# GpSimd makes the first weight sum of every up item that is made by quarter products

## The reference

```python
def swiglu(h, w13, w2):
    g, u = jnp.split(h @ w13, 2, axis=-1)
    return (jax.nn.silu(g) * u) @ w2

for l in range(DEPTH):
    h = modulated_norm(x, norm_w[l, 0], mod[:, 0])
    x = x + 0.5 * mod[:, 0, 2, None] * rmsnorm(swiglu(h, ffn_w13[l, 0], ffn_w2[l, 0]), norm_w[l, 1])
    ...
    h = modulated_norm(x, norm_w[l, 4], mod[:, 2])
    x = x + 0.5 * mod[:, 2, 2, None] * rmsnorm(swiglu(h, ffn_w13[l, 1], ffn_w2[l, 1]), norm_w[l, 5])
```

## Time and profile before

| | |
|---|---|
| median of 3 runs | 2648.08 us (2647.03 to 2648.61) |
| the profiled execution | 2643.59 us, span 2641.9 us |
| TensorE matmul busy | 2527.2 us, 96% |
| TensorE weight loads busy | 1893.2 us, 72% |
| VectorE busy | 1817.5 us, 69% |
| ScalarE busy | 516.6 us, 20% |
| GpSimd busy | 242.4 us, 9% |
| chain that ended last | TensorE 72%, VectorE 18%, DMA 3% |

### The profile page before, as it was taken

One profiled execution on the slowest core, in us unless ns is written; L12 is line 12 of the kernel. 1 busy time (PEld: TensorE's weight loads), 2 busy tenths in 40 slices (PEclk: granted clock), 3 DMA queues, 4 the chain that ended last, 5 costly groups with the idle time before them and its releaser, 6 DMA issues.

```text
span 2641.9 us, 69930 instructions
## 1 busy us (share of the span) xinstructions
PE 2527.2 (96%) x31413; PEld 1893.2 (72%) x31413; DVE 1817.5 (69%) x3017; ACT 516.6 (20%) x1053; POOL 242.4 (9%) x372
## 2 busy tenths in 40 slices
PE   7999999999999999999999999999999999999998
PEld 6984877877775455499579758787778745556993
DVE  4786455667785876479879865556787758664765
ACT  1000232212221332110010011322222223321000
POOL 6200101000001101010000010110010011010000
PEclk9999999999999999999999999999999999999999
DMA  9985433322235552398577654423222275435543
GB/s 362 323 298 176 136 114 104 118 86 94 94 109 198 177 192 96 127 314 282 197 255 276 223 173 142 157 86 104 100 89 86 95 242 171 172 112 178 197 160 127
DMA packets 239004, 445.34 MB, mean 169 GB/s; under 512 B 8920, under 2 KB 103702, under 8 KB 238704
## 3 DMA queue, kind: packets, MB, share of 16 engines
q1 hardware_dynamic: 224016, 395.60, 43.0%
q0 software_dynamic: 12960, 38.98, 4.6%
q10 hardware_dynamic: 1728, 6.29, 0.6%
HBM read 422.88 MB, written 17.96 MB: 167 GB/s over the span
## 4 chain that ended last, share of the span: by engine, by line
PE 72%; DVE 18%; DMA 3%; issue 3%; ACT 2%; SPq 1%; POOL 1%; DVEq 0%; POOLq 0%; ACTq 0%
PE ps L1230 71%; DVE scratch L2505 10%; DVE scratch L2511 3%; DMA ring<-in_ffn_w 2%; DVE scratch L2508 1%; DVE ring L2505 1%; DVE gbc L2511 1%; DMA scratch<-acs_scratch 1%; PE ps L1259 1%; DVE scratch L2937 1%; DVE x L2511 0%; DMA acs_scratch<-scratch 0%; ACT scratch L2149 0%; PE ps L1947 0%; DVE merged L2505 0%
## 5 line engine op out<-in xcount | busy, mean ns | idle before, releaser
L1230 PE MATMUL ps<-scratch 64*64 64x32 f32 (+6 forms) x15928 | 785.0, 245 | 62.2 <-DVE scratch L2505 27.6
L1230 PEld LDWEIGHTS ps<-scratch 64*64 64x64 f32 (+2 forms) x15928 | 635.3, 141 | 246.1 <-issue 116.3
L1230 PE MATMUL ps<-hT,ring 64*64 64x256 f32 (+3 forms) x8096 | 784.6, 356 | 9.5 <-issue 3.3
L1230 PEld LDWEIGHTS ps<-hT,ring 64*64 64x64 f32 (+2 forms) x8096 | 636.4, 155 | 89.5 <-issue 17.8
L1230 PE MATMUL ps<-ring,hT 64*64 64x256 f32 (+2 forms) x2816 | 425.4, 423 | 5.5 <-DVE scratch L2511 2.6
L2505 DVE TENSOR_TENSOR scratch<-scratch 128x256 f32<-128x256 f32 (+5 forms) x557 | 339.0, 609 | 108.7 <-ACTq L2313 31.8
L1230 PE MATMUL ps<-ring,scratch 128*128 128x512 f32 x864 | 394.1, 594 | 2.5 <-DVE scratch L2508 1.3
L1230 PEld LDWEIGHTS ps<-ring,hT 64*64 64x64 f32 (+1 forms) x2816 | 229.1, 150 | 142.8 <-issue 115.9
L1230 PEld LDWEIGHTS ps<-ring,scratch 128*128 128x128 f32 x864 | 158.3, 190 | 172.2 <-issue 166.6
L2505 DVE TENSOR_TENSOR scratch<-scratch,ps 128x512 f32<-128x512 f32 (+2 forms) x385 | 195.6, 508 | 116.3 <-PE ps L1230 89.7
L2511 DVE SCALAR_TENSOR_TENSOR scratch<-scratch,ccol 128x1024 f32<-128x1024 f32 x120 | 154.7, 1289 | 15.5 <-DMA scratch<-in_ada_w 11.4
(11 more groups left out here) (248 smaller groups left out, 1759.9 us busy)
## 6 DMA issues: line engine op xcount, KB each, us to landing
ring<-in_w_in SPq DMA_DIRECT2D x56, 2048.0 KB, 8.9
ring<-in_ffn_w SPq DMA_DIRECT2D x88, 1024.0 KB, 7.7
scratch<-in_ada_w SPq DMA_DIRECT2D x66, 1024.0 KB, 10.2
ring<-in_ffn_w SPq DMA_DIRECT2D x80, 512.0 KB, 5.6
ring<-in_w_branch_mamba SPq DMA_DIRECT2D x8, 2048.0 KB, 8.0
scratch<-acs_scratch POOLq DMA_DIRECT2D x24, 512.0 KB, 6.2
scratch<-fill_scratch SPq DMA_DIRECT2D x16, 512.0 KB, 8.5
ring<-in_w_branch_rwkv SPq DMA_DIRECT2D x4, 2048.0 KB, 10.8
```

The lines of the kernel that those rows point to most:

```text
L1230: return pe.matmul(o, lhsT, rhs, start=start, stop=stop)
```

## The change

GpSimd gets a helper, `first_weight_sums`, which for each item waits for the weights and, where the buffer was in use, for the quarter product m5 of item j - 2 that read it, then makes s1 = a21 + a22. VectorE waits for that instead of the weights and makes the three other sums. In GpSimd's order the calls stand: in block (l, 0) ahead of the roots of the norms (l, 2) and (l, 3), which in layer 0 is behind `constants()`; in block (0,1) two items behind `layer_parameters`, eight behind `layer_rows`; in block (1,1) all ten behind the load into `merged`.

```diff
+        first_sum_made = signal("first_sum_made", 0)
...
+            def first_weight_sums(l, f, js):
+
+                for j in js:
+                    item = ffn_item(f, j)
+                    par = item % 2
+                    w = ring[:, par, :].rearrange("p (k u n) -> p k u n", k=KT, u=2)
+                    pool.wait_ge(*slot_loaded[par](l, loads_before(item, par) + 2))
+                    if seven((l, f), j - 2):
+                        pool.wait_ge(*product(l, f, f"m5_{j - 2}"))
+                    pool.tensor_tensor(kset[j % 2][0], w[:, 0:KT // 2, 1, :], w[:, KT // 2:KT, 1, :], ALU.add).then_inc(first_sum_made.sem, 1)
...
                     last_gate_row(0)
                     constants()
+                first_weight_sums(l, 0, SEVEN[l, 0])
                 rstd((l, 2), (l, 3))
...
                     layer_parameters(l + 1)
+                    first_weight_sums(l, 1, SEVEN[l, 1][:2])
                     pool.wait_ge(*made(l, 1, "act_1"))
                     layer_rows(l + 1)
+                first_weight_sums(l, 1, SEVEN[l, 1][2 if l + 1 < DEPTH else 0:])
...
                 dve.wait_ge(*slot_loaded[par](l, loads_before(item, par) + 2))
-                own.step(tt(s1, a21, a22, ALU.add))
+                dve.wait_ge(*first_sum_made(0, seven_count(l, f, j)))
                 own.step(tt(a21, a11, a21, ALU.subtract))
```

More of the change, by code:

```diff
@@ L210, in up_count, with seven_count @@
     return sum(len(names(b)) for b in before) + names((l, f)).index(name) + 1
+def seven_count(l, f, j):
+    before = BLOCKS[:BLOCKS.index((l, f))]
+    return sum(len(SEVEN[b]) for b in before) + SEVEN[l, f].index(j) + 1
 def up_read(l, f, j):
```

## The result

The changed kernel takes 2662.03 us (median of 4, 2657.69 to 2663.93) where the kernel before takes 2647.56 beside it (4 runs, 2643.36 to 2648.61): ratio 1.0055, 95% interval 1.0041 to 1.0069, slower by 14.5 us. The prediction had 2663.0. The profiled execution took 2663.93, its span is 2661.9. In the rows PE is TensorE, PEld its weight loads, DVE VectorE, ACT ScalarE and POOL GpSimd.

The account below looks back on a forecast made before the run. The prediction took TensorE (96% busy) as the bound, with VectorE nearly in balance in the middle blocks' up phases. Terms 9.1 + 2.5 + 0.9 + 4 - 1.5 = +15.0 us on the median 2648.08 gave 2663 us, range 2654 to 2676.

Parts of the forecast that it names:

- Item 2's wait: Block (0,0), fourth quarter product of item 2: TensorE waits 9.1 us for a sum queued behind GpSimd's constants.
- The clock: Behind TensorE's wait at item 2 of (0,0): work at half clock speed costs 2.5 us.
- The end of (0,0): Down sums of block (0,0): the last item's sum comes later and VectorE passes it on, 0.9 us.
- Block (0,1): Block (0,1): item 1's wait plus collisions, less slack and what the last two give back, +4 us (-2.8 to +10).
- six of eight landings collide at +1.1 each: Items 3 to 10 of (0,1): six weight landings put GpSimd's addition on VectorE's pieces or weight sums, +1.1 us each.
- Item 1's own wait: Block (0,1), item 1: the sum waits behind GpSimd's parameter loads, costing TensorE 1 us.
- Block (1,0): Block (1,0): VectorE's load ends +1.0 over eight items, early savings go into the 2.7 us wait; -1.5 us.
- the good bound (-4.1): Block (1,0), favourable end of the range: the 2.7 us wait and its slow clock gone, -4.1 us.
- Block (1,1): Block (1,1): no pieces after the fourth item and TensorE doesn't wait, so 0 us.
- the constants stay slow: Rival, start of (0,0): constants don't speed up, wait 16.4 instead of 9.1 us, +22.3, 2670 us; chance 0.20.
- every addition collides: Rival, blocks (0,1) and (1,0): all 16 landings cost 1.1 us, +31, 2679 us; chance 0.08.
- VectorE relieved: Rival: VectorE keeps its pace beside GpSimd and its waits go, +4.0, 2652 us, within 0.2%; chance 0.10.

Follow-up runs that it names:

- e3: Changed kernel, but GpSimd makes item 2's sum of block (0,0) inside its building of constants, ahead of the fifth selecting step; 2650.86 us.
- e2: Kernel before, but GpSimd makes the first weight sum of item 2 of block (0,0) alone, the other 34 stay on VectorE; 2654.89 us.
- e4: Changed kernel, but GpSimd's sum for item 1 of block (1,0) waits until that block's first normalised tile is made; 2656.43 us.
- e11: Changed kernel, but for item 1 of block (1,0) GpSimd copies a21 instead of adding a21 and a22; no time given.
- e12: Changed kernel, but for item 1 of block (1,0) GpSimd fills the tile with zeros instead of adding; no time given.
- e1: Changed kernel, but VectorE again makes the first weight sum of item 2 of block (0,0), GpSimd keeps the other 34; 2651.09 us.
- e9: Changed kernel with item 2's sum made inside the constants and item 1's sum of (1,0) held until the normalised tile; 2645.77 us, ratio 1.0000.
- e10: Changed kernel, but GpSimd makes each sum as two halves of 128x512; 2662.30 us.

## Why the prediction was right, and where not

The forecast of +15.0 us met +14.5. For the largest term, item 2 and the clock behind it, that is earned: 11.6 in the sum, 12.8 by the rows. That the total is so close is luck: the terms of (0,1) and (1,0) erred by 5.4 and 2.2 us, in opposite directions; the steps add up to 13.7, and the interval of the measured difference is 11 to 18 us.

- **Item 2's wait, 9.1:** 9.6. The constants ended at 73.07 where I had 73.8, and the product could start at 79.63 where I had 80.2. The wait is longer all the same, as TensorE was ready at 70.0 in this execution and not at 71.13. Right, with its reason (e3 shows the slow selects coming back), within the 8.0 to 9.7 that the wait takes in e2, e4, e11 and e12.
- **The clock, 2.5:** 3.1 (6.17 us of matmuls at the half level). The bound taken from the earlier trace rows, 5.5 us at half speed, was too short by a little.
- **The end of (0,0), 0.9:** a step of 1.6, and 3.4 to 6.5 in the seven other kernels with these additions (e1, e3, e4, e9 to e12), where the wait is 2.4 to 4.7 and the clock drops too. The term was mis-sized: I counted the 1.1 us of the last item's later sum and set the earlier items at nothing behind their whole items. With them on GpSimd the last landing came 0.2 to 3 us later. The changed kernel's profile shows the smallest of these steps.
- **Block (0,1), +4:** -1.4, of which 1.0 is in e2 too. The step that failed is "six of eight landings collide at +1.1 each". Of items 3 to 10 three met an operation that they held (the additions at 1174.24, 1188.54 and 1251.58), none of them a weight sum; the other five fell on closing sums, which read PSUM, one of them on the end of a weight sum too, and lengthened none of these. In the block VectorE had 5.5 us less to do. Item 1's own wait was foreseen at 1 us and is 0.86. A collision at its worst is a little larger than I took it, 2.6 us and not 2.35, for instance on a group of four multiplications that takes 5.25 undisturbed:

```profile
1172.44 7.89 DVE L2532 SCALAR_TENSOR_TENSOR scratch<-scratch,ccol 128x1024 f32<-128x1024 f32 x4
...
1174.24 2.36 POOL L1046 TENSOR_TENSOR scratch<-ring 128x1024 f32<-128x1024 f32 x1
```

  My walk through the landings kept VectorE at the pace of before, while in fact each miss or hit moves it against the next one. That this is why fewer met such an operation is my reading; no run shows it.
- **Block (1,0), -1.5:** +0.7, from two parts. At its end -4.4, the good bound (-4.1) whole, against a load that I had growing by 1.0; over items 2 to 10 it fell by 3.8 (11.0 us of sums against four operations longer by 7.2). At its start +5.1, which the sum didn't have at all. In the list of what each addition could meet I only had VectorE's sums and pieces; item 1's addition stands directly behind the statistic and one transfer in GpSimd's queue, and the normalisation waits for that same statistic, so the two start together. Asking which of VectorE's operations GpSimd itself releases would have shown it.
- **Block (1,1), 0:** the shift stays at 20.2 to 20.3 us through it. Four of its ten additions hold VectorE, 6.1 us in all, and cost nothing.
- **The rivals.** That the constants stay slow (2670) fell with the pairs of 0.76 us. That every addition collides fell with 12 collisions of 35. VectorE relieved was half right: in (1,0) it is. The Trainium skill (SBUF — State Buffer, "Who interferes with whom") has the lock go to whichever of the two issues first, for the whole instruction. The cost of a collision agrees, and so does the other order, where VectorE's operation started first (the last section has a row). It also reads the selects otherwise than I did: where VectorE kept its 1.23 us, the selects had grown to 2.18, so it was GpSimd that was held there, and the rule was not broken. By the recorded starts, though, the normalisation began 0.46 us ahead of the addition, and lost.

## What to carry to other kernels

Before work is moved to an engine that looks idle, look where it stands in that engine's own queue at each moment, first of all in its start-up; one addition behind 12 us of constants cost more than the other 34 together. Then ask what VectorE operation starts at the same moment, above all one that this engine has just released: GpSimd's 2.35 us on a 0.75 us operation with TensorE waiting cost 5. And bound the gain first by leaving the work out: 43 us less on VectorE were worth 9 to TensorE, in two places, and only the nine additions that lead up to one of them were needed to take 3.

## What was not expected of the hardware

- A GpSimd instruction that only writes (0.97 us) holds VectorE's normalising TENSOR_SCALAR as one with two operands does. Between two back-to-back instructions of GpSimd (e10) VectorE got in where its operation started while the first ran, seven times, and did not where it started ahead of the first, twice. What makes the difference these runs don't show.
- VectorE's operation can be held though it starts ahead of GpSimd's by the records. In the changed kernel, e10, e11 and e12 the normalisation starts 0.43 to 0.46 us ahead of GpSimd's row and loses all the same (and so does the piece at 1173.76 in the changed kernel, 0.48 us ahead, also just behind a transfer of GpSimd's); the transfer that GpSimd issues just ahead takes 0.61 us there, and 1.03 or 1.04 in the kernel before and in e4, where nothing follows it and the normalisation takes its 0.75. Who gets in first is thus decided ahead of what the rows show; how stays open.
- The other way round GpSimd is the one that waits: selects of 0.76 us a pair take up to 2.66 beside VectorE's sums, which stay at 1.23. It does so with an addition too. In the changed kernel three additions took 2.61 to 2.97 us, each where an operation of VectorE with both operands in SBUF had started 0.02 to 0.48 us earlier and kept its length:

```profile
1210.53 1.23 DVE L2526 TENSOR_TENSOR scratch<-ring,scratch 128x1024 f32<-128x1024 f32 x1
1211.01 2.97 POOL L1046 TENSOR_TENSOR scratch<-ring 128x1024 f32<-128x1024 f32 x1 [9.05 <-DMA ring<-in_ffn_w]
```

- The clock was granted at half within or behind waits of TensorE of 9.63 and 4.09 us, of 3.39 (e1) and 2.44 (e3) at the down sums and of 2.7 in the earlier trace rows; behind the 2.31 of the changed kernel at the down sums it stayed up, but also behind 2.76 and 2.67 in e11 and e12 at the transposes. In a mixer the same wait of 1.94 or 1.95 us was followed by half speed in the kernel before (from 822.2) and by none in the changed one (at 834.6). The length of the wait alone doesn't tell; what was a fixed price in my sum is one that comes or doesn't.
